# Rows of local attention turned by VectorE blocks and DMA instead of TensorE, in the two layers of the second block

## The reference, cut to what matters

```python
def token_mixer(x, ...):
    q_a, k_a, v_a, x_m, z_m = split(x @ w_in)
    y_a = dilated_attention(q_a, k_a, v_a, rel_bias)      # 8 heads of 64, causal, softmax over <= 256 keys
    x_c = silu(causal_conv(x_m, conv_w, conv_b))          # 4 taps, 512 columns
    q_m, k_m = x_c @ w_qk_m[0], x_c @ w_qk_m[1]           # per head of 128, 4 heads
    v_m = x_m @ w_v_m
    gates = concat(q_m, k_m, v_m) @ w_if + b_if
    h = mlstm_chunkwise(q_m, k_m, v_m, i_pre, log_sigmoid(f_pre))
    y_m = sigmoid(z_m) * norm(h)
    g_a, g_m = split(sigmoid(x @ w_gate + b_gate))        # 8 gate slots
    return (g_a * (y_a @ w_br_a) + g_m * (y_m @ w_br_m)) @ w_o

x = layer_norm(ALPHA * x + token_mixer(x))
x = layer_norm(ALPHA * x + (swiglu(x) if layer 2 else moe_ffn(x)))   # layer 3: 8 experts of 3584, top 2
```

## Time and profile before

| | |
|---|---|
| time, median of 3 runs | 2236.96 us (2236.05 to 2237.69) |
| time of the profiled execution | 2238.39 us |
| its span, first to last instruction | 2237.0 us |
| TensorE products, busy | 2217.7 us, 99% |
| VectorE busy | 1760.3 us, 79% |
| ScalarE busy | 1364.5 us, 61% |
| mean granted TensorE clock | 0.998 of full speed |

### The profile page before, as it was taken

How to read it: one execution, slowest core, us unless ns; L and a number is a source line. 1 busy time by engine, 2 the same in 40 slices (tenths; PEclk the granted TensorE clock), 3 DMA queues, 4 the chain that set the end, 5 groups by cost and what they waited for, 6 DMA issues and landing times.

```text
span 2237.0 us, 30263 instructions
## 1 busy us (share of the span) xinstructions
PE 2217.7 (99%) x12156; PEld 1904.7 (85%) x12156; DVE 1760.3 (79%) x2253; ACT 1364.5 (61%) x1764; POOL 167.5 (7%) x231
## 2 busy tenths in 40 slices
PE   9999999999999999999999999999999999999997
PEld 7998888998888999888899887888888888888886
DVE  7976656977564588665678898999999998989898
ACT  5654444655443454444455577777777777877775
POOL 3100111300120000211100010000000000000001
PEclk9999999999999999999999999999999999999999
DMA  8455764546763535776625699999999999999996
GB/s 279 151 191 212 240 233 154 176 170 215 246 235 132 185 132 208 245 236 205 226 93 187 249 349 406 386 380 388 376 382 382 386 370 386 373 392 360 390 372 251
DMA packets 104163, 611.39 MB, mean 273 GB/s; under 512 B 24056, under 2 KB 25384, under 8 KB 34896
## 3 DMA queue, kind: packets, MB, share of 16 engines
q1 hardware_dynamic: 80496, 568.76, 67.3%
q0 software_dynamic: 9872, 31.12, 4.0%
q10 hardware_dynamic: 13648, 9.50, 1.6%
HBM read 591.07 MB, written 18.62 MB: 273 GB/s over the span
## 4 chain that ended last, share of the span: by engine, by line
PE 96%; DVE 3%; DMA 1%; ACT 0%; issue 0%; SPq 0%; POOL 0%; DVEq 0%
PE bank L491 28%; PE bank L493 28%; PE bank L492 28%; PE bank L488 8%; DVE wl L1662 2%; PE bank L768 1%; PE bank L721 1%; PE bank L521 1%; DMA spare<-in_ws 1%; DMA raw<-in_ws 0%; PE bank L816 0%; PE bank L1088 0%; DVE TU L1873 0%; DVE EL L1689 0%; ACT wh L1189 0%
## 5 line engine op out<-in xcount | busy, mean ns | idle before, releaser
L1662 DVE TENSOR_TENSOR wl<-raw,wh 128x1024 fp32r<-128x1024 f32 x698 | 819.9, 1223 | 219.9 <-ACT wh L1189 216.7
L1189 ACT ACTIVATE wh<-raw 128x1024 fp32r<-128x1024 f32 x704 | 704.3, 1052 | 331.1 <-PE bank L493 295.2
L491 PE MATMUL bank<-wh,GH 128*128 128x512 f32 x896 | 352.8, 394 | 0.0
L493 PE MATMUL bank<-wh,GL 128*128 128x512 f32 x896 | 349.3, 390 | 0.0
L492 PE MATMUL bank<-wl,GH 128*128 128x512 f32 x896 | 348.8, 389 | 0.0
L1662 DVE TENSOR_TENSOR wl<-spare,wh 128x1024 fp32r<-128x1024 f32 x264 | 309.8, 1221 | 26.8 <-ACT wh L1189 25.3
L1189 ACT ACTIVATE wh<-spare 128x1024 fp32r<-128x1024 f32 x264 | 264.2, 1054 | 61.0 <-PE bank L493 56.9
L491 PE MATMUL bank<-HH,wh 128*128 128x256 f32 x832 | 239.6, 288 | 0.1
L492 PE MATMUL bank<-HL,wh 128*128 128x256 f32 x832 | 235.3, 283 | 0.0
L493 PE MATMUL bank<-HH,wl 128*128 128x256 f32 x832 | 235.2, 283 | 0.0
L491 PE MATMUL bank<-wh,HH 128*128 128x512 f32 (+1 forms) x600 | 223.4, 372 | 0.0
(11 more groups left out here) (319 smaller groups left out, 3537.1 us busy)
## 6 DMA issues: line engine op xcount, KB each, us to landing
raw<-in_ws SPq DMA_DIRECT2D x352, 1024.0 KB, 6.6
spare<-in_ws SPq DMA_DIRECT2D x132, 1024.0 KB, 7.1
more<-in_ws SPq DMA_DIRECT2D x48, 1024.0 KB, 5.0
scratch_blocks<-TB POOLq DMA_DIRECT2D x30, 256.0 KB, 2.9
TURNED<-scratch_blocks POOLq DMA_DIRECT2D x36, 128.0 KB, 4.8
once<-in_ws SPq DMA_DIRECT2D x4, 1024.0 KB, 11.4
scratch_parts<-Y POOLq DMA_DIRECT2D x7, 512.0 KB, 8.5
REL<-in_relb ACTq DMA_DIRECT2D x4, 768.0 KB, 13.3
```

What stands on the lines that cost most here:

```text
L491: T.q.matmul(o, l[0], r[0], start=start, stop=False)
L493: return T.q.matmul(o, l[1], r[0], start=False, stop=stop)
L1189: A.q.activation(sets[c % NSET][0][:, half * i:half * i + half], raws[stream.place[n]][:, half * i:half * i + half], ACT.Copy).then_inc(*h ...
L1662: V.q.tensor_tensor(wl[:, half * i:half * i + half], raw[:, half * i:half * i + half], wh[:, half * i:half * i + half].bitcast(f32), ALU.s ...
```

## The change

- In layers 2 and 3, `v_even_blocks` takes the place of `v_even`. It writes the divided rows to `PT` in another order of 32-column blocks, and two VectorE transposes of 32 x 32 blocks write them back to `LB[t]`. `g_turn_p` then lets GpSimd's queue write `LB[t]` to DRAM in two transfers and read it back with the blocks in their turned places in four. `t_block_outputs` multiplies straight from `LB[t]`. TensorE's 24 transposes and the six bank copies (three on each of ScalarE and VectorE) are gone.
- The value products of tile 1 move from ahead of the projections to behind the transposes of v. The first half of gate 3 moves from behind mk to between mv and mq, the second half from behind the transposes of v to ahead of the gates' inputs. ScalarE's `a_gate(l, 3)` and both engines' output copies of tile 1 move accordingly.
- A convolution is cut in two: its last multiply (`v_conved`) is issued behind the next head's convolution.
- There are five `once` buffers instead of four. `once0` is the bias table, free after layer 3's last scores; `once1` is free after the recurrent output of layer 3, `once2` and `once3` after its last `wo` product, `once4` as all four were before. The load of the last norm's factors (1 MB) into the bias table moves behind expert 1.

```diff
-        more, once, spare = ["more0", "more1"], ["once0", "once1", "once2", "once3"], ["spare0", "spare1"]
+        more, once, spare = ["more0", "more1"], [f"once{i}" for i in range(5)], ["spare0", "spare1"]
...
-        for i, a in enumerate((0, 2048, 4096, 14336)):
-            raws[f"once{i}"] = at(f"once{i}", a, SLOT)
+        raws["once0"] = nc.alloc_sbuf_tensor_at("once0", [128, SLOT], f32, offset=arena_at + 4 * 22016)
+        for i, a in enumerate((4096, 0, 2048, 14336)):
+            raws[f"once{i + 1}"] = at(f"once{i + 1}", a, SLOT)
...
+        def t_block_outputs(l, a, t, kts, v, ready, turned=False):
+            room = groups.take(T, "to", l, a, t)
+            P = LB[t][:, 0:1024 * kts].rearrange("p (b x q) -> p x b q", b=4, q=32)
+            T.wait_ge(*p_in[t].at(l, a, 3))
+            for c in range(4):
+                for i in range(kts):
+                    T.wait_ge(*ready(i))
+                    for p in range(2):
+                        weights_t = P[:, (2 * c + p) * kts + i]
+                        if turned:
+                            weights_t = weights_t[:, ::-1, ::-1]
+                        ins = t_mm(room[64 * p:64 * p + 64, 128 * c:128 * c + 128].rearrange("p (b q) -> p b q", b=4),
+                                   v(2 * c + p, i), weights_t, i == 0, i == kts - 1)
+            ins.then_inc(*groups.fill("to", l, a, t))
...
             t_gate(l, 0)
             t_gate(l, 1)
-            t_turn_p(l, "c", 0, 8, 1, even)
             t_gate(l, 2, (0,))
-            t_outputs(l, "c", 0, 1, v_c, lambda i: out("v", l, i), True)
-            t_turn_p(l, "c", 1, 8, 2, even)
+            t_block_outputs(l, "c", 0, 1, v_c, lambda i: out("v", l, i), True)
             t_gate(l, 2, (1,))
-            t_outputs(l, "c", 1, 2, v_c, lambda i: out("v", l, i), True)
...
             heads("mv", lambda h: wv[:, h, :], XM, lambda h: out("xm", l, h // 2))
+            t_gate(l, 3, (0,))
             heads("mq", lambda h: wqk[:, h, :], XC, lambda h: xc.at(l, h))
             heads("mk", lambda h: wqk[:, 4 + h, :], XC, lambda h: xc.at(l, h))
-            t_gate(l, 3, (0,))
+            t_gate(l, 3, (1,))
...
-            t_gate(l, 3, (1,))
+            t_block_outputs(l, "c", 1, 2, v_c, lambda i: out("v", l, i), True)
...
+        def v_even_blocks(l, a, t, n):
+            su, kts = sm[f"su{a}{t}"], n // 128
+            turned = PT[:, 0:8 * n].rearrange("p (b r x k) -> p r x b k", b=4, r=2, k=32)
+            for r in range(2):
...
+                V.q.tensor_tensor(turned[:, r], P,
+                                  rz[:, :, None, None].to_broadcast([128, 4 * kts, 4, 32]),
+                                  ALU.mult).then_inc(*evened.mark(l, a, t, r))
+            V.wait_ge(*evened.at(l, a, t, 1))
+            for g in range(2):
+                own = slice(4 * n * g, 4 * n * g + 4 * n)
+                V.q.transpose(LB[t][:, own], PT[:, own]).then_inc(*p_blocked.mark(l, a, t, g))
...
             v_scores(l, "c", 1, 256, lambda h: BIAS[:, 256 * h:256 * h + 256])
-            v_even(l, "c", 1, 256)
+            v_even_blocks(l, "c", 1, 256)
             v_gate(l, 0)
             v_conv(l, 0)
-            v_turn_p(l, "c", 0, 8, 1)
             v_gate(l, 1)
             v_conv(l, 1)
+            v_conved(l, 0)
             v_conv(l, 2)
+            v_conved(l, 1)
+            v_conv(l, 3)
+            v_conved(l, 2)
             v_turn_o(l, "c", 0, OA[1])
-            v_turn_p(l, "c", 1, 8, 2)
-            v_conv(l, 3)
-            v_turn_o(l, "c", 1, OA[1])
+            v_conved(l, 3)
             v_scale_x("wo", l)
             v_gate(l, 2)
             v_lo(s + MLSTM + 2)
...
             v_copy(VT[:, 512:1024], ("mvt", l, 1), 512)
+            v_turn_o(l, "c", 1, OA[1])
             V.wait_ge(*full("ift", l))
...
+        def g_turn_p(l, a, t, kts):
+            w = 1024 * kts
+            for g in range(2):
+                G.wait_ge(*p_blocked.at(l, a, t, g))
+                G.q.dma_start(bass.AP(turned_p.tensor, 262144 * t + w // 2 * g, [[w, 128], [1, w // 2]]),
+                              LB[t][:, w // 2 * g:w // 2 * g + w // 2]).then_inc(*p_out[t].mark(l, a, g))
+            G.wait_ge(*p_out[t].at(l, a, 1))
+            for b in range(4):
+                G.q.dma_start(LB[t][32 * b:32 * b + 32, 0:w].rearrange("p (q n) -> p q n", q=4),
+                              bass.AP(turned_p.tensor, 262144 * t + w // 4 * b,
+                                      [[w, 32], [32 * w, 4], [1, w // 4]])).then_inc(*p_in[t].mark(l, a, b))
...
-            elif r.startswith("once"):
+            elif r == "once0":
+                S.wait_ge(*out("sc", 3, "c", 1, 3))
+            elif r == "once1":
+                S.wait_ge(*turned.at(3, 1))
+            elif r in ("once2", "once3"):
+                S.wait_ge(*full("wo", 3, 1, 1))
+            elif r == "once4":
                 S.wait_ge(*normed.at(7, 1, 1))
```

More of the change, by code:

```diff
@@ L297, in program @@
     blocks = nc.dram_tensor("scratch_blocks", (6, 2 * 128 * 512), f32).ap()
+    turned_p = nc.dram_tensor("scratch_p", (2, 2, 128 * 1024), f32).ap()
     stream = Stream()
@@ L328, in program @@
         PICK = sb("PICK", 128)
+        RZX = sb("RZX", 16)
         SENT = sb("SENT", 4, mybir.dt.int32)
@@ L477, in program @@
         blocks_in = [signal(f"blocks{i}_in", 16) for i in range(2)]
+        p_blocked = signal("p_blocked")
+        p_out, p_in = ([signal(f"p_{n}{t}", 16) for t in range(2)] for n in ("out", "in"))
         flag, select, selr, yhi, ydone = (signal(n) for n in ("flag", "select", "selr", "yhi", "ydone"))
@@ L924, in v_c @@
                 return QT[:, 2048 + 512 * i + 64 * h:2112 + 512 * i + 64 * h]
-            def even(l, a, t, h):
-                return evened.at(l, a, t, h // 4)
             def ready_c(h):
@@ L1476, in a_block_two @@
             a_hi(gate_slot(l, 3))
-            a_turn_p(l, "c", 0, 8, 1)
             a_gate(l, 1)
@@ L1480, in a_block_two @@
             a_conv(l, 2)
+            a_conv(l, 3)
             a_turn_o(l, "c", 0, OA[1])
-            a_turn_p(l, "c", 1, 8, 2)
             a_gate(l, 2)
-            a_conv(l, 3)
-            a_turn_o(l, "c", 1, OA[1])
             a_hi(s + MLSTM + 2)
@@ L1489, in a_block_two @@
             a_copy(KM[:, 0:512], ("mk", l, 0), 512, 0.5)
+            a_gate(l, 3)
             a_copy(VT[:, 0:512], ("mvt", l, 0), 512)
+            a_turn_o(l, "c", 1, OA[1])
             A.wait_ge(*forget.at(l))
@@ L1495, in a_block_two @@
             a_hi(gate_slot(l, 5))
-            a_gate(l, 3)
             a_hi(gate_slot(l, 6))
@@ L1509, in a_block_two @@
             a_gate(l, 5)
+            A.wait_ge(*p_blocked.at(l, "c", 1, 1))
             a_turn_p(l, "m", 0, 4, 1)
@@ L1538, in a_router @@
             A.wait_ge(*top.at(3, "c", 1))
-            A.q.dma_start(BIAS[:, 0:2048], bass.AP(ln_d.tensor, 3 * 2048, [[0, 128], [1, 2048]])
-                          ).then_inc(*ln_in.mark(8))
         def a_gates():
@@ L1598, in a_experts @@
                         later[j - 3]()
+                if e == 1:
+                    A.wait_ge(*lo_of(EXPERTS + 2).at(EXPERTS + 2, 1))
+                    A.q.dma_start(BIAS[:, 0:2048], bass.AP(ln_d.tensor, 3 * 2048, [[0, 128], [1, 2048]])
+                                  ).then_inc(*ln_in.mark(8))
                 if e < 7:
@@ L1998, in v_even @@
                                   ALU.mult).then_inc(*evened.mark(l, a, t, r))
+        def v_even_blocks(l, a, t, n):
+            su, kts = sm[f"su{a}{t}"], n // 128
+            turned = PT[:, 0:8 * n].rearrange("p (b r x k) -> p r x b k", b=4, r=2, k=32)
+            for r in range(2):
+                own = slice(4 * r, 4 * r + 4)
+                rz = RZX[:, 8 * r:8 * r + 4 * kts]
+                P = LB[t][:, 1024 * r:1024 * r + 1024]
+                P = P.rearrange("p (x b k) -> p x b k", b=4, k=32) if kts == 2 else (
+                    P.rearrange("p (x b k) -> p x b k", b=8, k=32)[:, :, 0:4])
+                V.wait_ge(*raised.at(l, a, t, 4 * r + 3))
+                if a == "a":
+                    V.wait_ge(*sink_exp.at(l, t))
+                    V.q.tensor_tensor(su[:, own], su[:, own], sm[f"es{a}{t}"][:, own], ALU.add).then_inc(*step.mark())
+                    V.wait_ge(*step.now())
+                V.q.reciprocal(rz.rearrange("p (h i) -> p h i", h=4),
+                               su[:, own][:, :, None].to_broadcast([128, 4, kts])).then_inc(*step.mark())
+                V.wait_ge(*step.now())
+                V.q.tensor_tensor(turned[:, r], P,
[5 more added lines that the diff above has]
+                V.q.transpose(LB[t][:, own], PT[:, own]).then_inc(*p_blocked.mark(l, a, t, g))
         def v_turn_p(l, a, t, heads, kts):
@@ L2123, in v_conv, with v_conved @@
                 ins.then_inc(*(step.mark() if d < 3 else conved.mark(l, h)))
+        def v_conved(l, h):
+            c = XC[:, 256 * h:256 * h + 256]
             V.wait_ge(*tanhed.at(l, h))
@@ L2144, in v_block_two @@
```

(4 more changed lines are left out.)

## The result

| | before | after |
|---|---|---|
| median, 5 runs each | 2236.96 us (2236.05 to 2239.69) | 2247.38 us (2245.45 to 2249.56) |
| profiled execution, its span | 2238.39, 2237.0 | 2247.38, 2246.1 |
| mean granted clock | 0.998 | 0.996 |

The ratio is 1.0045, interval 1.0033 to 1.0057: the changed kernel is slower by 0.45%, against 0.27% forecast. The measured 2247.38 us lies outside the likeliest case's own range (2239.4 to 2244.4) and inside that of the rival in which the clock falls (2244.5 to 2249).

The account below looks back on a forecast made before the run. TensorE's products, 99% of the span, were taken to bound the kernel. A layer: - 2.5 + 4.8 + 0.7 = + 3.0, so + 6.0 in two: 2243.0 us against the median 2236.96, range 2239.0 to 2248.5.

Parts of the forecast that it names:

- the likeliest case: Whole kernel: TensorE waits in layers 2 and 3 but the clock stays up; 2239.4 to 2244.4 us, chance 0.45.
- the rival in which the clock falls: Rival, TensorE at gate 3: the wait lowers the granted clock, giving 2244.5 to 2249 us; chance 0.28.
- the removal: TensorE in layers 2 and 3: transposes of the rows of tiles 0 and 1 go, saving 2.51 us a layer.
- the late bias: VectorE: the gates' bias addition starts later behind tile 1's output copy, costing 0.7 us a layer (bounds 0 and 0.9).
- the rival of 0.28: Rival, TensorE at gate 3: the granted clock falls in the wait, at most + 3.0 us a wait; chance 0.28.
- The wait at gate 3: TensorE before gate 3's first half waits 4.8 us a layer for VectorE's rest of slot 14 (bounds 3.7 and 5.3).
- The clock: TensorE behind the wait: a fall to half speed, nothing in the forecast, as rival up to + 3.0 us a wait; chance 0.28.
- The early slots: First expert: loading its first slots sooner gains 0 us (bounds 2.7 us saved or 1 us lost).
- The rival of 0.12: Rival, first expert: the early slots pay and the 2.73 us hole goes, giving 2240.3 us; chance 0.12.
- The round trip: Rows through DRAM and back: covered, costs nothing; as rival, tile 1 late by 11 us a layer, 2265 us, chance 0.05.
- VectorE in time: Rival, gate 3: slot 14's rest is ready at 1160.4, so no wait, and the time is 2233.4 us; chance 0.10.

Follow-up runs that it names:

- e7_last_multiply_first: e2_bias_first with VectorE's multiply for the fourth head put ahead of tile 0's output copy; 2232.07 us, 0.9975 of the kernel before.
- e1_rest_early: The changed kernel with slot 14's rest made on VectorE ahead of the convolutions and ScalarE's part ahead of the first tanh; 2234.23 us, 0.9985 of the kernel before.
- e6_gate3_back: The changed kernel with both halves of gate 3 back behind mk on TensorE; 2236.88 us, 0.9997 of the kernel before.
- e2_bias_first: e1_rest_early with VectorE's output copy of tile 1 put behind the gates' bias addition and absolute value; 2233.42 us, 0.9978 of the kernel before.
- e4_filled_wait: The changed kernel with 16 unread 512-column products on TensorE ahead of gate 3's first half in each layer; 2242.91 us, 1.0021 of the kernel before.
- e3_scale_behind: The changed kernel with VectorE's scaling of X put behind slot 14's rest instead of ahead of it; 2244.12 us, 1.0027 of the kernel before.
- e5_slots_alone: The kernel before with only the five once buffers, their waits and the moved norm load; 2237.36 us, 0.9998 of the kernel before.
- e8_values_back: e2_bias_first with tile 1's value products back between gate 2's second half and mv, output copies moved back too; 2246.04 us, 1.0034 of the kernel before.

## Why the prediction was right, and where it was short

*What held and what did not.* The wait, its place and its cause came as worked out, and so did the removal and the late bias. The likeliest case, in which the clock stays up, had 0.45 and did not come; the rival of 0.28 came, with its price inside its bounds.

*The removal.* 2.5 us a layer was right: with every wait but small ones taken away (e7_last_multiply_first) the layers gave 5.1 us, against 5.0 worked out. The value products kept their price, 1.03 us for tile 0 and about 1.9 for tile 1, so reading four runs of 32 columns cost nothing here.

*The wait at gate 3.* Forecast 4.8 us, measured 4.53 in both layers, in the place and from the releaser named; from start to start, with mv at its old 1.70, it is 1170.36 - (1163.94 + 1.70) = 4.7 in layer 3:

```profile
1163.94 1.89 PE L493 MATMUL bank<-U,raw 128*128 128x256 f32 x8
```

The 1024-wide transposes take 2.37 us for two (1.2 each assumed), and the output copy waited 0.63 us for ScalarE (forecast 1162.0 - 1161.3 = 0.7). That it was VectorE's order and not its load is shown by e1_rest_early and, from TensorE's side, by e6_gate3_back.

*The late bias.* Forecast 0.7 us a layer, measured 0.7 by e2_bias_first. In the changed kernel's layer 3 the norm's transposes come 1213.94 - 1204.14 = 9.8 us late: the 0.4 from ahead of layer 2 and all that the two layers lose.

*The clock.* This is the term that was mis-sized. The prediction left it at nothing in the likeliest case and made it a rival with 0.28, "+ 3.0 a wait" at most and half of that in the time given. It fell at both waits and cost 3.7 us, 1.85 a wait, which e4_filled_wait shows by itself. There are two errors in it. The prediction's own row (4.1 us) was already shorter than its own wait (4.8), so by its own numbers the fall was the likelier case, and 0.28 was too low. And the row was one place only, the end of the execution: e3_scale_behind shows the fall 2.0 us after the last product. The Trainium skill, TensorE: Matmul & The Clock Gate, Part 1, says that the default state is throttled and activity releases the throttle. The traces of these waits agree: in each the clock comes back only when products have run again for some microseconds, 3.4 to 6.8 us after its fall.

*The early slots.* Taken as 0, measured 0 (e5_slots_alone). The rival of 0.12, 2.7 us, lies outside the interval.

*The round trip.* Covered, as costed: e6_gate3_back has no wait for it. In the changed kernel GpSimd issues tile 1's first write 1.5 us after the transposes begin and its four reads from 1159.96; e8_values_back shows the price without cover, 4.2 us a layer and the clock. The warning of the Trainium skill, VectorE: DVE Perf Modes, The three transpose paths, of slow transposes by strides did not bear on it: reads of 256 KB in runs of 2 KB landed in 5.7 us (median, layer 3). No run here has a transposing DMA, so its factor is not tested.

*VectorE in time* was out by 4.5 us. The sum: - 5.0 + 9.1 + 1.4 + 3.7 = + 9.2, against + 9.4 in the layers. The medians are 10.4 apart, 1.0 more than the layers; that last microsecond is placed nowhere and is within their spread.

## What to carry to other kernels

When work is taken from the engine that bounds, what stands behind it comes due earlier by as much, and by more if its order is changed too: list, for each block that moves forward, the last item in another engine's list that it needs, and work out that item's time. Here two instructions of VectorE at the wrong end of its list, with the clock's fall that followed, cost 12 us in the two layers, and moving them, with ScalarE's rounded part that they need, made the same change faster than the kernel before.

Holes of 3.4 to 4.5 us in this stream of products cost themselves and mostly some 2 us more; those of 1 to 3 us cost the more only in some traces. Where such a hole can't be avoided, products that nobody reads can keep the clock: 4.0 us of them in a wait of 4.8 did, and cost nothing that shows. They have to be shorter than the wait.

A busy share of 99% on both sides said nothing: the chain's shares and the rows with a releaser did.

## What the runs showed of the hardware

The granted clock fell in or right behind waits of 3.4, 4.2 and 4.5 us in all six cases traced (two layers in each of three kernels), but at different points: 2.0 us after the last product in e3_scale_behind's layer 3, 2.5 in the changed kernel's layer 2, only when the wait of 4.5 us was over in its layer 3, and 1.0 us behind the end of the wait in e8_values_back's layer 3. It does not fall in every execution: e3_scale_behind's mean clocks, above, say so for waits of 3.4 us.

Behind shorter holes it fell in some traces only. In the first expert's hole (of the weight loads), 1.1 to 2.7 us in nine traces, it fell in two: e7_last_multiply_first (2.3 us) and e8_values_back (2.6), and not in the kernel before (2.7) or the six others. The windows of e7_last_multiply_first at that place, and of e5_slots_alone behind layer 3, columns as above:

```profile
1349.00:1351.50 2.50, 0.62 (x4) 0.20 (x2) 2.50 (x5) 2.25 (x4) 0.59 (x1) 1.00 1.03 433
1351.50:1352.00 0.50, 0.50 (x3) 0.50 (x4) 0.50 (x1) 0.50 (x1) 0.00 (x0) 0.66 0.99 393
1352.00:1355.00 3.00, 3.00 (x10) 2.42 (x9) 3.00 (x4) 2.49 (x4) 0.00 (x0) 0.50 1.00 419
1355.00:1355.50 0.50, 0.50 (x4) 0.41 (x3) 0.50 (x2) 0.00 (x0) 0.00 (x0) 0.93 1.06 442
```

```profile
1265.00:1270.00 5.00, 4.02 (x29) 3.75 (x29) 4.13 (x14) 0.65 (x2) 0.00 (x0) 0.89 0.74 306
1270.00:1275.00 5.00, 5.00 (x32) 4.87 (x32) 5.00 (x6) 4.23 (x8) 0.00 (x0) 0.76 0.22 51
```

In the second, the holes of the two windows together come to 5.00 - 4.02 = 0.98 us, and the clock was still low for (0.11 + 0.24) x 5 / 0.5 = 3.5 us. The kernel before has holes of the same length there, 0.45 and 0.52 us, and kept the clock. So the length of a hole does not settle it: two of half a microsecond were once followed by a fall, one of 2.7 us was not, and even 3.4 us is not sure to bring it. What else decides stays open.

How long products then ran at 1.2 GHz varied as well, from 3.4 us to about 6. Half of that is lost, so by this estimate two executions of one kernel may differ by a microsecond or two from this alone.
